# A block of eleven matrix products on one core: the first token half's normalised tiles are formed during the second half's pass, and five orders are changed

## The reference

```
x = x + even_layer(x)      # z = rmsnorm(x) @ w_in: conformer convolution (31 taps) * silu(gate), and
                           # 8 heads of causal attention: (softmax(q k^T) v) * silu(b_gate); both @ w_out
x = x + odd_layer(x)       # z = rmsnorm(x) @ w_in -> cq, ckv, ik, iw, gate;  cq, ckv = rmsnorm (latents)
                           # index scores pick 64 keys a token, 16 heads attend to ckv; o * silu(gate) @ w_out
x = rmsnorm(x)
x = x + [gated_delta_rule(...), short_conv(...)] @ w_mix_out   # chunks of 64 tokens, a state of 8 heads
x = x + cross_attention(rmsnorm(x), rmsnorm(mem)) @ w_xo
x = x + (silu(conv(h w_gate)) * conv(h w_up)) @ w_ffn_down;  out = rmsnorm(x)
```

## Time and profile before

| | |
|---|---|
| median of 3 runs | 2539.49 us (2538.24 to 2540.8) |
| the profiled execution | 2537.43 us |
| its span, first to last instruction | 2535.7 us |
| PE busy | 2469.4 us, 97% of the span |
| PE's share of the chain that ended last | 90% (DVE 6%, ACT 2%) |
| DVE, ACT busy | 1648.7 us (65%), 1187.3 us (47%) |
| granted TensorE clock, mean | 0.993 |

### The profile page before, as it was taken

One profiled execution on the slowest core, in us unless ns is written; L12 is line 12 of the kernel. 1 busy time (PEld: TensorE's weight loads), 2 busy tenths in 40 slices (PEclk: granted clock), 3 DMA queues, 4 the chain that ended last, 5 costly groups with the idle time before them and its releaser, 6 DMA issues.

```text
span 2535.7 us, 34643 instructions
## 1 busy us (share of the span) xinstructions
PE 2469.4 (97%) x13691; PEld 2130.5 (84%) x13691; DVE 1648.7 (65%) x2003; ACT 1187.3 (47%) x1415; POOL 159.2 (6%) x149
## 2 busy tenths in 40 slices
PE   7999999999999999999999999999999999999998
PEld 6888888887878788888888888888888888888887
DVE  6998775556775776595556545445777557755764
ACT  5434664445464653642355445334655334433433
POOL 1000000000200100000000000000022002110220
PEclk9999999999999999999999999999999999999999
DMA  7654446544426465552026555435455555655644
GB/s 239 199 188 152 158 165 209 165 145 133 152 90 208 133 198 162 172 166 100 1 100 232 166 199 183 149 133 199 156 180 194 199 189 175 198 187 183 195 164 151
DMA packets 343491, 422.86 MB, mean 167 GB/s; under 512 B 14654, under 2 KB 269388, under 8 KB 342860
## 3 DMA queue, kind: packets, MB, share of 16 engines
q1 hardware_dynamic: 340396, 411.40, 49.4%
q0 software_dynamic: 2512, 8.45, 1.1%
q10 hardware_dynamic: 464, 1.32, 0.2%
HBM read 419.05 MB, written 2.10 MB: 166 GB/s over the span
## 4 chain that ended last, share of the span: by engine, by line
PE 90%; DVE 6%; ACT 2%; issue 1%; DMA 0%; POOL 0%; SPq 0%; ACTq 0%; DVEq 0%
PE ps L732 34%; PE ps L733 17%; PE ps L778 9%; PE ps L780 9%; PE ps L779 9%; PE ps L1041 3%; DVE w_lo L2021 1%; ACT w_hi L1319 1%; PE ps L735 1%; PE ps L736 1%; PE ps L737 1%; PE ps L968 1%; PE ps L1238 1%; PE ps L1229 1%; PE ps L1005 1%
## 5 line engine op out<-in xcount | busy, mean ns | idle before, releaser
L732 PE MATMUL ps<-h_cat,w_hi 128*128 128x512 f32 x3840 | 1363.1, 400 | 10.6 <-DVE h_cat L2162 4.6
L733 PE MATMUL ps<-h_cat,w_lo 128*128 128x256 f32 x3840 | 1076.1, 280 | 0.0
L732 PEld LDWEIGHTS ps<-h_cat,w_hi 128*128 128x128 f32 x3840 | 723.1, 188 | 189.2 <-issue 12.0
L733 PEld LDWEIGHTS ps<-h_cat,w_lo 128*128 128x128 f32 x3840 | 726.9, 189 | 2.2 <-issue 1.9
L2021 DVE TENSOR_TENSOR w_lo<-ring,w_hi 128x2048 fp32r<-128x2048 f32 (+2 forms) x281 | 589.9, 2101 | 198.2 <-ACT w_hi L1319 195.4
L1319 ACT ACTIVATE w_hi<-ring 128x2048 fp32r<-128x2048 f32 (+2 forms) x281 | 493.9, 1759 | 88.4 <-PE ps L780 62.9
L2017 DVE TENSOR_TENSOR w_lo<-ring,w_hi 128x2048 fp32r<-128x2048 f32 (+1 forms) x136 | 302.9, 2232 | 231.6 <-ACT w_hi L1316 228.6
L1316 ACT ACTIVATE w_hi<-ring 128x2048 fp32r<-128x2048 f32 (+1 forms) x136 | 252.6, 1862 | 271.6 <-PE ps L780 246.9
L778 PE MATMUL ps<-w_hi,h_cat 128*128 128x512 f32 x640 | 250.7, 392 | 1.8 <-DVE w_lo L2017 1.8
L780 PE MATMUL ps<-w_hi,h_cat 128*128 128x512 f32 x640 | 249.2, 389 | 0.0
L779 PE MATMUL ps<-w_lo,h_cat 128*128 128x512 f32 x640 | 249.1, 389 | 0.0
(11 more groups left out here) (430 smaller groups left out, 2428.5 us busy)
## 6 DMA issues: line engine op xcount, KB each, us to landing
ring<-in_w_ffn_up SPq DMA_DIRECT2D x44, 2048.0 KB, 8.0
ring<-in_w_mix_in SPq DMA_DIRECT2D x28, 2048.0 KB, 8.3
ring<-in_even_w_in SPq DMA_DIRECT2D x27, 2048.0 KB, 8.1
ring<-in_w_ffn_down SPq DMA_DIRECT2D x16, 2048.0 KB, 8.1
ring<-in_odd_w_in SPq DMA_DIRECT2D x11, 2048.0 KB, 8.3
ring<-in_even_w_out SPq DMA_DIRECT2D x8, 2048.0 KB, 8.0
ring<-in_odd_w_out SPq DMA_DIRECT2D x8, 2048.0 KB, 7.9
ring<-in_w_mix_out SPq DMA_DIRECT2D x8, 2048.0 KB, 8.1
```

Source lines behind the costliest of these rows:

```text
L732: mm(o[:, 0:2 * T], whi[slot][:, k, :], flat(cat[:, k]), start=first, stop=False)
L733: ins = mm(o[:, T:2 * T], wlo[slot][:, k, :], cat[:, k, 0, :], start=False, stop=end)
```

## The change

It has seven parts.

1. **Norms 1, 2, 5.** The first token half's four scaled quarters are all formed by VectorE (`first_half`), each in a place of its own. TensorE transposes them in the middle of the second pass (`turn_ahead`, 16 transposes), ScalarE and VectorE form hi and lo of half 0 in the same time (`hi_ahead`, `first_half`). After the pass TensorE runs 6, 10 and 6 matmuls whose result nobody reads, then 16 transposes of half 1, then the first unit with no transposes in it. Hi and lo of half 1 are formed in the order `HALF_ORDER`. One split of weights less stands ahead on VectorE and one less on ScalarE.
2. **`gain1`** (the final norm's gain) lies elsewhere and is loaded later; VectorE waits for it at its first use.
3. **Heads of the even layer.** The division of a head's probabilities follows its exp in the same turn of the loop instead of the next. `e_bgate` is drained by a plain copy; silu is applied to two heads at a time.
4. **Latents.** `orq` is inverted in two halves, the second one turn later.
5. **`o_gate1`.** VectorE sums before it splits (`sums_first`).
6. **Delta section.** `a_t` stands ahead of the last unit's sum and that sum behind `low`; `log_diff` behind the first `v_new`; the state's decay is a step of its own behind both `v_new`.
7. **`g_out`.** The lo part of its third unit stands ahead of `o_gate`.

```diff
@@ Steps.__init__ @@
-            ahead = {(0, "w_state"): (0, decays[0:1]), (0, "o_copy"): (0, decays[1:2]), (0, "state"): (0, decays[2:4]),
-                     (1, "v_new"): (0, decays[4:5]), (1, "o_state"): (1, decays[0:1]), (1, "o_copy"): (1, decays[1:2]),
+            ahead = {(0, "w_state"): (0, decays[0:1]), (0, "o_copy"): (0, decays[1:2]),
+                     (1, "st_decay"): (0, decays[4:5]), (1, "o_state"): (1, decays[0:1]), (1, "o_copy"): (1, decays[1:2]),
                      (1, "state"): (1, decays[2:5])}
...
+                        if (t, j, stage[1], hh) == (0, 1, "v_new", 0):
+                            for early in decays[2:4]:
+                                add(*early, 1, 0)
...
@@ places @@
-    gain1 = place("gain1", [P, D], off=H_OFF + 20 * KB)
+    gain1 = place("gain1", [P, D], off=AR)
...
@@ gpsimd @@
-        pool.wait_ge(sem["o_drained"], A_ODD + DSA_HEADS)
+        pool.wait_ge(sem["h_ready"], H_GROUPS["gate"] + 4)
         pool.dma_start(gain1[:], a["final_norm"].unsqueeze(0).to_broadcast([P, D])).then_inc(sem["gain1_loaded"], 16)
...
@@ tables of the norms @@
+    HALF_ORDER = (0, 2, 4, 6, 1, 3, 5, 7)
...
@@ tensor: unit @@
-                    k = (step + TURNS[norm][1]) % g.kt
+                    k = 2 * HALF_ORDER[step // 2] + step % 2 if norm in HALVED else (step + TURNS[norm][1]) % g.kt
...
-                if norm is not None and step % 2 == 1 and step // 2 + 4 < 8 and not TURNS[norm][2]:
+                if norm is not None and step % 2 == 1 and step // 2 + 4 < 8 and not TURNS[norm][2] and norm not in HALVED:
...
@@ tensor: wide_seg, rows_apart @@
+                        if norm is not None and t and j == g.units - 2:
+                            turn_ahead(norm)
...
@@ tensor: turn_half removed @@
+        def turn_quarter(norm, c):
+            o = TURNS[norm][0][c]
+            for i in range(4):
+                ins = nc.tensor.transpose(o[:, i * P:(i + 1) * P], xs[:, c % 2, c // 2, i * P:(i + 1) * P], ident[:])
+            return ins
+        def turn_ahead(norm):
+            for c in range(4):
                 pe.wait_ge(sem["scaled_dve"], 4 * scaled_at[norm] + c + 1)
...
+                turn_quarter(norm, c).then_inc(sem["turned_half"], 1)
         def turn_first(norm):
             if norm in HALVED:
-                for p in range(4):
-                    turn_half(norm, p, 0)
-                for p in range(4):
-                    turn_half(norm, p, 1).then_inc(sem["turned"], 1)
+                for n in range({1: 6, 2: 10, 5: 6}[norm]):
+                    mm(ps[n % 2][:, 0:T], ident[:], causal[:, 0, :], start=True, stop=True)
+                for c in range(4):
+                    if c % 2:
+                        pe.wait_ge(sem["scaled_act"], 4 * scaled_at[norm] + c + 1)
+                    else:
+                        pe.wait_ge(sem["scaled_one"], 2 * HALVED[norm] + c // 2 + 1)
+                    pe.wait_ge(sem["half_ready"], 4 * HALVED[norm] + c + 1)
+                    turn_quarter(norm, c).then_inc(sem["turned"], 2)
...
@@ tensor: the three norms (odd_norm; likewise mix_norm, ffn_norm) @@
-        wide_seg("e_out", tiles_ready=H_GROUPS["qe"], rows_apart=True)
+        wide_seg("e_out", tiles_ready=H_GROUPS["qe"], rows_apart=True, norm=1)
...
@@ scalar: drain of e_bgate @@
-                ins = af(bg[:, at_j, :].rearrange("p a t -> p (a t)"), src, ACT.Silu)
+                ins = af(bg[:, at_j, :].rearrange("p a t -> p (a t)"), src, ACT.Copy)
...
@@ scalar: norms @@
+        def hi_ahead(k, g):
+            act.wait_ge(sem["row_ready"], g.w0 + 4)
+            ...
+                ins.then_inc(sem["half_hi"], 1)
+        def hi_rest(k, n):
+            p = HALF_ORDER[n]
+            act.wait_ge(sem["turned"], 8 * norm_at[k] + 2 * (p // 2) + 2)
+            if n >= 4:
+                act.wait_ge(sem["ht_ready"], 8 * norm_at[k] + n - 3)
+            ...
+            ins.then_inc(sem["ht_hi"], 1)
         def halved_rows(k, roots, free, sources):
             act.wait_ge(sem["rstd_ready"], roots)
-            for c in range(5):
-                if 1 <= c < 4:
-                    scaled(k, sources[c], c, 2 if c == 1 else 1)
+            for c in (1, 3):
+                act.wait_ge(sem["turned_half"], 4 * HALVED[k] + c + 1)
+                af(xs[:, 1, c // 2, :], sources[c], ACT.Copy, scale=tok_rstd[:, 1:2]).then_inc(sem["scaled_act"], 2)
                 if c == 1:
                     act.wait_ge(sem["acc_ready"], free.n0 + free.units)
-                if c >= 1:
-                    hi(k, 2 * c - 2), hi(k, 2 * c - 1)
+                for n in (0,) if c == 1 else range(1, 8):
+                    hi_rest(k, n)
         def halved_norm(k, roots, halves, g, then):
            table_for_roots()
             square_row(g, 0)
             root_of(0, "half_totalled", halves, "half_std")
-            split_to(S[then].n0 + 3)
+            split_to(S[then].n0 + 1)
+            hi_ahead(k, g)
+            split_to(S[then].n0 + 2)
...
@@ scalar: e_heads_beside @@
-                if 4 <= u_ < 4 + HEADS:
-                    exp_step(u_ - 4)
                 if 6 <= u_ < 6 + HEADS:
                     h = u_ - 6
                     pt_step(h, pe_pt, ps[4 + h % 2], sem["o_ready"], h)
+                if 5 <= u_ < 5 + HEADS and u_ % 2:
+                    h = u_ - 5
+                    act.wait_ge(sem["drained"], S["e_bgate"].f0 + h + 2)
+                    af(bg[:, h:h + 2, :], bg[:, h:h + 2, :], ACT.Silu).then_inc(sem["bg_ready"], 1)
+                if 4 <= u_ < 4 + HEADS:
+                    exp_step(u_ - 4)
...
@@ vector: seg (with sums_first for o_gate1) @@
+                if sums_first:
+                    post_to(g.n0 + j + 1 - LAG)
                 split_to(g.n0 + j + 1)
                 post_to(g.n0 + j + 1 - LAG)
...
@@ vector: norms @@
+        def first_half(k, then):
+            for c in range(4):
+                nc.vector.tensor_scalar(xs[:, c % 2, c // 2, :], x[:, 0, c * WIDE:(c + 1) * WIDE], tok_rstd[:, 0:1], None,
+                                        ALU.mult).then_inc(sem["scaled_dve"], 1)
+            split_to(S[then].n0 + 1)
+            for c in range(4):
+                dve.wait_ge(sem["half_hi"], 4 * HALVED[k] + c + 1)
+                for i in range(4):
+                    ins = stt(h_lo[:, 4 * c + i, 0:P], TURNS[k][0][c][:, i * P:(i + 1) * P], col(NORMS[k], 4 * c + i),
+                              h_hi[:, 4 * c + i, 0:P].bitcast(F32), ALU.mult, ALU.subtract)
+                ins.then_inc(sem["half_ready"], 1)
+        def second_half(k):
+            for n, p in enumerate(HALF_ORDER):
+                dve.wait_ge(sem["ht_hi"], 8 * norm_at[k] + n + 1)
+                ...
+                ins.then_inc(sem["ht_ready"], 1)
...
@@ vector: halved_norm (likewise for the norm of g_qkv) @@
-            scaled(k, x, 0)
-            scaled(k, x, 1)
-            split_to(S[then].n0 + 2)
+            first_half(k, then)
             add_row(g, 1)
             total_of(1, SQUARES[k]).then_inc(sem["totalled"], 1)
             inverse_of(1, "std_ready", roots, tok_rstd).then_inc(sem["rstd_ready"], 1)
             dve.wait_ge(sem["rstd_ready"], roots)
-            one_scaled(k, x)
-            turned_rows(k, x)
+            two_scaled(k)
+            second_half(k)
...
@@ vector: e_heads_beside @@
-                if 5 <= u_ < 5 + HEADS:
-                    scale_step(u_ - 5)
+                    scale_step(u_ - 4)
                 if 7 <= u_ < 7 + HEADS:
                     h = u_ - 7
                     dve.wait_ge(sem["o_ready"], h + 1)
-                    dve.wait_ge(sem["drained"], S["e_bgate"].f0 + h + 1)
+                    dve.wait_ge(sem["bg_ready"], h // 2 + 1)
...
@@ vector: key_beside @@
-                ch.link(nc.vector.reciprocal(orq[:], orq[:]))
+                ch.link(nc.vector.reciprocal(orq[:, 1, :], orq[:, 1, :]))
...
+            if 4 * i + b == 4:
+                ch.link(nc.vector.reciprocal(orq[:, 0, :], orq[:, 0, :]))
...
@@ vector: v_new @@
-            ins = tt(g_["vn"][r], g_["u"][r], b4(A(hh))[r], ALU.subtract)
-            if (t, j) == (1, 1):
-                return ins
+            return tt(g_["vn"][r], g_["u"][r], b4(A(hh))[r], ALU.subtract)
+        def st_decay(t, j, hh):
+            after(dve, "w_state", t, j, hh)
             hs = slice(4 * hh, 4 * hh + 4)
...
         def state_step(t, j, hh):
             after(dve, "o_state", t, j, hh)
+            after(dve, "st_decay", t, j, hh)
...
@@ vector: delta section @@
-        post_to(S["g_b"].n0 + 8)
+        post_to(S["g_b"].n0 + 7)
+        dve.wait_ge(sem["acc_ready"], S["g_b"].n0 + 6)
+        for hh in range(2):
+            go("a_t", 0, hh)
...
+            if (name, key) == ("low", (0, 1)):
+                post_to(S["g_b"].n0 + 8)
+            if (name, key) == ("o_scale", (1,)):
+                split_to(S["g_out"].n0 + 3)
...
```

(74 more changed lines are left out.)

26 lines of the change are left out of this document (17 added, 9 removed).

## The result

The changed kernel took 2526.07 us as the median of four runs (2522.35 to 2528.28), the kernel before 2540.14 us beside it: a ratio of 0.9944, 95% interval 0.9927 to 0.9961. That is 14 us faster where 24 were forecast, and 2 us above the range. The profiled execution took 2528.03 us, span 2526.3, so it is 9.4 us shorter than that of before.

A forecast was written before the change was run, and what follows sets the result against it. TensorE was taken as the bound, 97% busy. Terms of 26.1 us less 2.0 for the clock, 24.1, off the profiled 2537.43 gave 2513.3; with 2.1 from profile to median, 2515.4 us, range 2508 to 2524.

The forecast's parts named there:

- the 2.0 that were set for it: Heads: 2.0 us given back of the upper end of 7.3, for serial mask, exp and division, leaving 5.3.
- Part 1(e): Norms: VectorE splits the second unit's weights (2.29 us) only behind sixteen subtractions; a new wait, second unit at about 11.5 us.
- The clock in the norms: Norms 1, 2 and 5: TensorE's clock counted on to fall in one of the three, -2.0 us of gain.
- Rival A: Clock falls in all three norms: gain less by 6.2 us than forecast, 2521.6 us; chance 0.17.
- the range's lower end: No clock falls (2513.4), plus the heads' whole 7.3, 0.3 per norm and part 5's 1.3: about 5 lower, 2508 us.
- Rivals B: Loop of heads becomes the bound; small waits at eight heads eat the 5.3 but 1: 2519.7 us; chance 0.15.
- C: Waits only move, each engine waiting elsewhere for the same work: 2537 to 2539 us; chance 0.05.
- D: Slower than before: low clock at the norms not left again within the first unit, 2541 us or more; chance 0.03.

The follow-up runs named there:

- Experiments 1: Changed kernel with the lo split of the second unit's weights of g_qkv and f_up0 ahead of the second half's subtractions: 2517.88 us.
- 5: Kernel before with parts 1 and 2 alone (three norms and gain1): 2540.74 us, ratio 1.0007.
- 6: Kernel before with parts 1 and 2, and the second unit's lo split of g_qkv and f_up0 ahead of the second half's subtractions: 2530.97 us.
- 9: Changed kernel with each drain and sum of g_qkv and f_up0 ahead of the split that stood before it on ScalarE and VectorE: 2518.34 us.
- Experiment 2: Changed kernel with the squares, root and scaling of the memory rows each one unit of g_out later: 2522.94 us.
- orders_only: Kernel before with parts 4 to 7 alone (latents, o_gate1, delta section, g_out): 2529.04 us, ratio 0.9964.
- experiment 3: Changed kernel without the 6, 10 and 6 matmuls that nobody reads: 2530.21 us, ratio 0.9968.
- norms_only: The same run as 5: kernel before with parts 1 and 2 alone: 2540.74 us, ratio 1.0007.

## Why the prediction was wrong

**The gains (parts 1, 3 to 7)** were right step by step: no gain is off by more than 0.8 us. The heads gave back the 2.0 that were set for it, at `pe_pt`, `ag` and the convolution's squares. The three norms gained 1.2, 2.45 and 2.45 to their first units, for 1.3, 1.7 and 2.2.

**Part 1(e), the failed step.** "A new wait, and it sets the second unit's start": the split behind the subtractions was priced by the unit that needs its weights. That wait was 0.18 us. The price lay in what the split frees: a ring buffer, so a load, so ScalarE's queue, so a drain. The term was missing, -4.9 and -5.0 us. Experiments 1, 5, 6 and 9 show it. The rows that would have told it were in the trace of before: the loads take some 8 us, and the drain follows the split in each loop.

**Part 7, the failed step.** "L778 waits 1.8 for a `w_lo` that now stands ahead: 1.8." The wait went and the time came back three units later. TensorE arrived 1.8 us earlier at a chain (load of the memory, squares, split) that had been just hidden, and the moved split put `h_cat`, and with it the load, 0.85 us later. With its half clock it is -3.4 in this profile, so part 7 lost 1.3; where the load took 9.5 to 9.7 us the wait alone was 3.05 to 3.28. Experiment 2 shows the chain, and orders_only that it does not hang on the norms.

**The clock in the norms.** -2.0 was set for one of three; none fell. Rival A is out: the clock falls in the norms only when the unread matmuls are taken away, and then in two of three (experiment 3). The clock did fall in the second chunk, -1.6, behind waits that have not changed; the same kernel's other profile does not show it, and of all 13 profiles 8 do. That term is luck, not the change. That no norm fell gave back the 2.0, so the miss is smaller than the missing terms.

**Slips in the working.** The span less TensorE's busy time is 66.3 us and not 58; 58.4 is the sum of the idle times ahead of its instructions. The distances given for the range's lower end add to 4.2 and not 5. Neither changes the forecast.

**The range** had no room for the pace: -3.0 in this profile, with the two profiles of one kernel 2.3 us apart by it. Together 26.1 + 0.9 (gains above forecast) - 13.3 - 1.6 - 3.0 is some 9, the profiled difference of 9.4.

Rivals B, C and D did not come about: though C, "each engine waits elsewhere for the same work", is what norms_only did, with 5.7 us of new waits for `stage` where 7.6 for `xs` had been.
